# Two RWKV / mLSTM / sparse-attention layers on one core: waits of the feed-forward leads and of the RWKV projections rearranged

## What is computed

```python
for l in range(DEPTH):                                   # 2
    h = h + 0.5 * rms(swiglu(rms(h, g[0]), ffn_w_in[l, 0], ffn_w_out[l, 0]), g[1])
    u = rms(h, g[2])
    p_rw, p_ml, p_dsa, p_gate = split(u @ w_in[l])
    y_rw  = rwkv7_mixer(p_rw, ...)                        # lerp with the previous token, LoRAs, recurrence
    y_ml  = mlstm_mixer(p_ml, ...)
    y_dsa = dsa_mixer(p_dsa, ...)
    mixed = sum(sigmoid(p_gate) * (y @ w_branch[l])) @ w_out[l]
    h = h + rms(mixed, g[3])
    h = h + 0.5 * rms(swiglu(rms(h, g[4]), ffn_w_in[l, 1], ffn_w_out[l, 1]), g[5])
return h[:, 16:]
```

## Time and profile before

| | us |
|---|---|
| median of three timed runs | 3420.24 |
| lowest and highest | 3418.71, 3427.62 |
| profiled execution, its own time | 3413.78 |
| its span in the profile | 3412.1 |
| TensorE busy | 3272.8 |
| VectorE, ScalarE, GpSimd busy | 1475.8, 1178.8, 1193.5 |

### The profile page before, as it was taken

One profiled execution on the slowest core, in us unless ns is written; L12 is line 12 of the kernel. 1 busy time (PEld: TensorE's weight loads), 2 busy tenths in 40 slices (PEclk: granted clock), 3 DMA queues, 4 the chain that ended last, 5 costly groups with the idle time before them and its releaser, 6 DMA issues. The chain is left out here.

```text
span 3412.1 us, 72944 instructions
## 1 busy us (share of the span) xinstructions
PE 3272.8 (96%) x29406; PEld 3003.0 (88%) x29406; DVE 1475.8 (43%) x2548; ACT 1178.8 (35%) x2251; POOL 1193.5 (35%) x906
## 2 busy tenths in 40 slices
PE   8999999999899999999999999999898989999998
PEld 8999989987688999999999999999776868878886
DVE  6332155345767434332053311454467673353312
ACT  3222242224554334222232223513245543332222
POOL 4444345110002443444444443352000124534442
PEclk9999999998999999999999999999899999999999
DMA  3333222002111332333223332220021213323332
GB/s 101 89 92 89 79 69 69 5 9 56 42 51 39 85 93 70 90 92 88 80 84 89 92 90 85 63 62 4 18 54 39 59 29 98 87 81 94 93 94 70
DMA packets 464405, 236.48 MB, mean 69 GB/s; under 512 B 20862, under 2 KB 462476, under 8 KB 464156
## 3 DMA queue, kind: packets, MB, share of 16 engines
q1 hardware_dynamic: 464156, 232.92, 24.4%
HBM read 230.50 MB, written 2.10 MB: 68 GB/s over the span
## 5 line engine op out<-in xcount | busy, mean ns | idle before, releaser
L579 POOL TENSOR_TENSOR W_low<-W,W_high 128x512 fp32r<-128x512 f32 (+1 forms) x544 | 725.2, 1335 | 868.6 <-ACT W_high L659 867.8
L155 PE MATMUL PS<-u_high,W_high 128*128 128x264 f32 (+1 forms) x2832 | 864.1, 305 | 8.5 <-DVEq L458 3.4
L156 PE MATMUL PS<-u_low,W_high 128*128 128x264 f32 (+1 forms) x2832 | 857.9, 303 | 0.0
L157 PE MATMUL PS<-u_high,W_low 128*128 128x264 f32 (+1 forms) x2832 | 857.7, 303 | 0.0
L659 ACT ACTIVATE W_high<-W 128x512 fp32r<-128x512 f32 (+1 forms) x544 | 336.0, 619 | 997.0 <-PE PS L157 943.6
L155 PEld LDWEIGHTS PS<-u_high,W_high 128*128 128x128 f32 x2832 | 533.2, 188 | 37.1 <-issue 6.3
L156 PEld LDWEIGHTS PS<-u_low,W_high 128*128 128x128 f32 x2832 | 533.7, 188 | 21.5
L157 PEld LDWEIGHTS PS<-u_high,W_low 128*128 128x128 f32 x2832 | 531.7, 188 | 21.7
L155 PE MATMUL PS<-u_high,dW_high 128*128 128x264 f32 (+1 forms) x1344 | 408.3, 304 | 12.4 <-POOL dW_low L1745 5.0
L157 PE MATMUL PS<-u_high,dW_low 128*128 128x264 f32 (+1 forms) x1344 | 386.1, 287 | 0.0
L156 PE MATMUL PS<-u_low,dW_high 128*128 128x264 f32 (+1 forms) x1344 | 386.0, 287 | 0.0
(11 more groups left out here) (399 smaller groups left out, 5333.5 us busy)
## 6 DMA issues: line engine op xcount, KB each, us to landing
W<-in_ffn_w_in SPq DMA_DIRECT2D x352, 256.0 KB, 2.9
dW<-in_w_in SPq DMA_DIRECT2D x172, 256.0 KB, 2.9
W<-in_ffn_w_out SPq DMA_DIRECT2D x160, 256.0 KB, 2.8
W<-in_w_in SPq DMA_DIRECT2D x80, 256.0 KB, 3.0
W<-in_w_branch SPq DMA_DIRECT2D x48, 256.0 KB, 2.9
W<-in_w_out SPq DMA_DIRECT2D x32, 256.0 KB, 2.8
W<-in_ffn_w_out SPq DMA_DIRECT2D x32, 128.0 KB, 2.2
xt<-in_x SPq DMA_DIRECT2D x4, 512.0 KB, 4.7
```

The lines of the kernel that those rows point to most:

```text
L155: nc.tensor.matmul(dst, wh, xh, start=first, stop=False)
L156: nc.tensor.matmul(dst, wh, xl, start=False, stop=False)
L157: return nc.tensor.matmul(dst, wl, xh, start=False, stop=final)
L579: g.tensor_tensor(WL[:, r, 0:nk], W[:, r, 0:nk], WH[:, r, 0:nk].bitcast(F32), ALU.subtract).then_inc(S("split"), 1)
```

## The change

In the feed-forward lead the banks of the sums and of the spread factors change places, tile 2 is made before the wait for the sums, and the third and fourth high halves are made behind the first and second k in place of ahead of them. In the RWKV projections the last eight tiles use four pairs of banks, the memsets come before the first low half, the kappa sums come four blocks (one unit) later, and PE waits for the fourth kappa scaling ahead of tile 15's last unit and the rest. The turn of the small tile, its copies and its transfer move into the first chunk of the recurrence, with bank 4 in place of bank 0; the slice function is renamed `at`.

```diff
@@ phase_ffn
-                lead = Lead(st, [hid[:, 0], hid[:, 1]], pre, (4, 6, 0), True)
+                lead = Lead(st, [hid[:, 0], hid[:, 1]], pre, (6, 4, 0), True)
...
                         pe.sem_inc(dve_evac, 4)
+                        tile(0, 2)
                         pe.wait_ge(S("sums_read"), 1)
-                        tile(0, 2)
                         tile(0, 3)
...
                         def first_high(act, k):
-                            for n in {None: (0, 1, 2, 3), 5: (4,), 6: (5,), 7: (6,)}.get(k, ()):
+                            for n in {None: (0, 1), 0: (2,), 1: (3,), 5: (4,), 6: (5,), 7: (6,)}.get(k, ()):
                                 high(n, n // R, n % R, 4)
@@ phase_rwkv, projections
-            dense = Dense(early, ..., columns, None, (4, 6, 2, 0) + (4, 6) * 10,
+            dense = Dense(early, ..., columns, None, (4, 6, 2, 0) + (4, 6) * 6 + (2, 0, 4, 6) * 2,
                           True, size=4)
...
                 def _(g):
-                    for u in range(8):
-                        dense.low(g, u)
                     g.memset(s3[:], 1.0).then_inc(S("starts"), 1)
                     g.wait_ge(S("starts"), 1)
                     g.memset(full(s3)[:, :, :, 0:1], 0.0)
                     g.memset(s3[:, :, NFULL * CH:NFULL * CH + 1], 0.0).then_inc(S("starts"), 1)
-                    for u in range(8, dense.all_units):
+                    for u in range(dense.all_units):
                         dense.low(g, u)
...
                     dense.blocks(pe, 4)
                     dense.blocks(pe, 4)
+                    dense.blocks(pe, 4)
                     pe.wait_ge(S("kappa_squares"), 1)
                     pe.wait_ge(S("sigmoid"), 8)
                     token_sums(lambda m: s4[:, m], per_parity, 2).then_inc(S("kappa_sums"), 1)
-                    dense.blocks(pe, 24)
+                    dense.blocks(pe, 20)
                     for m in range(4):
                         spread_out(m)
                         dense.blocks(pe, 8)
+                    pe.wait_ge(S("kappa_scaled"), 4)
                     dense.blocks(pe, KD * dense.tiles - dense.given)
-
-                    pe.wait_ge(S("d_out"), dense.tiles)
-                    pe.wait_ge(S("kappa_scaled"), 4)
-                    for j, (t0, n) in enumerate(QT):
-                        last = nc.tensor.transpose(PS[0:n, 0, 16 * j:16 * j + 16], small[64:80, t0:t0 + n],
-                                                   ident[64:80, 64:80])
-                    last.then_inc(S("small_turned"), 1)
@@ phase_rwkv, recurrence (the transfer and the two copies leave the projections too)
+                @block.sync
+                def _(sp):
+                    sp.wait_ge(S("small_turned"), 1)
+                    sp.dma_start(small[64:P], small[0:64]).then_inc(loaded2, 16)
+                    sp.wait_ge(loaded2, 16)
...
                             tt(za[:], near[:, :, 0], eye2[:].unsqueeze(1).broadcast_to([P, 4, 64]), ALU.add).then_inc(S("first_factor"), 1)
+                            if g == 0:
+                                v.wait_ge(S("small_turned"), 1)
+                                nc.vector.tensor_copy(tok[0:N_META, 0], PS[0:N_META, 4, 0:16])
+                                nc.vector.tensor_copy(tok[:, 1:5], PS[:, 4, 16:80].rearrange("p (j c) -> p j c", c=16)
+                                                      ).then_inc(S("small_out"), 1)
                             v.wait_ge(S("reach_made"), g + 1)
...
                         if p:
                             pe.wait_ge(S("x2"), p)
+                        else:
+                            pe.wait_ge(S("small_out"), 1)
...
                         if makes:
                             near_grams(g)
+                        if g == 0:
+                            turn_small()
                         if steps:
                             read(p)
```

More of the change, by code:

```diff
@@ L969, in phase_rwkv @@
                 ((0, C_KIDX, 72), (72, C_IG, 8))]
-            dense = Dense(early, w_in[ds(l, 1)].rearrange("a (k p) n -> p (a k) n", p=P), columns, None, (4, 6, 2, 0) + (4, 6) * 10,
+            dense = Dense(early, w_in[ds(l, 1)].rearrange("a (k p) n -> p (a k) n", p=P), columns, None, (4, 6, 2, 0) + (4, 6) * 6 + (2, 0, 4, 6) * 2,
                           True, size=4)
@@ L983, in _ @@
                         dense.load(sp, u)
-                    sp.wait_ge(S("small_turned"), 1)
-                    sp.dma_start(small[64:P], small[0:64]).then_inc(loaded2, 16)
-                    sp.wait_ge(loaded2, 16)
                 @block.gpsimd
                 def _(g):
-                    for u in range(8):
-                        dense.low(g, u)
                     g.memset(s3[:], 1.0).then_inc(S("starts"), 1)
@@ L1084, in _ @@
                         scaled(i)
-                    v.wait_ge(S("small_turned"), 1)
-                    nc.vector.tensor_copy(tok[0:N_META, 0], PS[0:N_META, 0, 0:16])
-                    own(nc.vector.tensor_copy(tok[:, 1:5], PS[:, 0, 16:80].rearrange("p (j c) -> p j c", c=16)))
                 @block.scalar
@@ L1239, in phase_rwkv @@
             LEN = [min(CH, T - g * CH) for g in range(NG)]
-            tok = lambda g: slice(g * CH, g * CH + LEN[g])
+            at = lambda g: slice(g * CH, g * CH + LEN[g])
             rows = lambda q, n: slice(64 * q, 64 * q + n)
@@ L1368, in grams @@
                                 for q in range(2):
-                                    last = mm(dst(m, k)[rows(q, n), 0:n], lhs[rows(q, 64), m, tok(g)],
-                                              rhs[rows(q, 64), m, tok(g)])
+                                    last = mm(dst(m, k)[rows(q, n), 0:n], lhs[rows(q, 64), m, at(g)],
+                                              rhs[rows(q, 64), m, at(g)])
                         return last
@@ L1377, in product, with turn_small @@
                         return last
+                    def turn_small():
+                        for j, (t0, n) in enumerate(QT):
+                            last = nc.tensor.transpose(PS[0:n, 4, 16 * j:16 * j + 16], small[64:80, t0:t0 + n],
+                                                       ident[64:80, 64:80])
+                        last.then_inc(S("small_turned"), 1)
                     def near_grams(g):
@@ L1395, in read @@
                             for q in range(2):
-                                last = mm(rps[rows(q, n), m], p_[rows(q, 64), m, tok(p)], state[rows(q, 64), s, m],
+                                last = mm(rps[rows(q, n), m], p_[rows(q, 64), m, at(p)], state[rows(q, 64), s, m],
                                           start=False)
@@ L1456, in turns @@
                                 for q in range(2):
-                                    last = mm(dst[rows(q, n), m], src[rows(q, 64), m, tok(g)], eye2[rows(q, 64)])
+                                    last = mm(dst[rows(q, n), m], src[rows(q, 64), m, at(g)], eye2[rows(q, 64)])
                         last.then_inc(S("turned"), 1)
@@ L1501, in outputs @@
                             for q in range(2):
-                                last = mm(yps[rows(q, 64), m, 0:n], state[rows(q, 64), s, m], r_[rows(q, 64), m, tok(p)],
+                                last = mm(yps[rows(q, 64), m, 0:n], state[rows(q, 64), s, m], r_[rows(q, 64), m, at(p)],
                                           start=False)
```

## The result

| | before | changed |
|---|---|---|
| median, us | 3420.24 (3417.41 to 3427.74, five runs) | 3395.59 (3386.33 to 3401.44, five runs) |
| ratio to before, 95% | | 0.9915 (0.9899 to 0.9931), 29 us faster |
| profiled execution, its span | 3413.78, 3412.1 | 3399.08, 3397.4 |
| TensorE busy | 3272.8 us, 96% | 3278.0 us, 96% |

A forecast was written before the change was run, and what follows sets the result against it. TensorE (PE), busy 96% of the span, was taken as the bound, so only its waits and slow clock could be won. Terms 3.4 + 10.1 - 0.5 + 2.2 + 2.8 + 5.6 + 2.4 = 26.0 us off 3420.2 gave 3394, range 3386 to 3406.

The forecast's parts named there:

- rival 1: Whole kernel: the forecast itself holds, 3394 us with its own range of 3387 to 3400; chance 0.50.
- Sums' banks: Feed-forward lead: tile 2 no longer waits for VectorE to read the sums; 4 x 0.86 = 3.4 us won.
- the margin of 1.8 us: Feed-forward lead: weights for tile 3's second half are ready 1.8 us before PE asks, however early the lead ends.
- Order of first splits: Feed-forward lead: two splits before the first `u_high` instead of four; 3 x 2.25 + 3.4 = 10.1 us won.
- without the wait I expect it to stay up: Very first feed-forward lead: without the 1.8 us wait the clock holds, adding 1.7 us for 3.4 in all.
- its lower end: Very first feed-forward lead: only the earlier PE start counts, 1.7 us instead of 3.4, without the clock gain.
- Memsets: RWKV stage start: GpSimd's memsets hold VectorE up 0.65 us in layer 2, save 0.1 twice; -0.5 us net.
- Kappa sums: RWKV projections: one 2.9 us unit goes ahead and covers PE's 1.1 us wait for the squares, twice; 2.2 us won.
- Bank pairs: Late RWKV projections: four pairs remove tile 19's 1.4 us wait per layer, GpSimd's low halves just keeping ahead; 2.8 us won.
- Small turn: End of RWKV projections: PE restarts at the recurrence 2.8 us sooner in each of two layers; 5.6 us won.
- The clock term: Recurrence restart: clock holds after a 1.5 us idle stretch, 1.5 won less 0.3 for transposes; net 1.2 a layer, 2.4 us.
- a gain under 14 us would prove the sum wrong in more than a size: Whole kernel: the prediction's own failure test, set against its summed gain of 26.0 us.

The follow-up runs named there:

- the second comparison: The changed kernel itself, timed again beside its feed-forward and RWKV halves, against the kernel before on the same chip: median 3391.73 us, ratio 0.9906.
- the idle stretch put back: The changed kernel plus a 128 KB transfer reloading unread weights, with a wait, at the end of the RWKV projections: 3403.23 us, against 3421.09 for the kernel before.

## Why the prediction was right, point by point

The forecast case, rival 1 of the list, is what happened: 3394 forecast, 3395.59 measured. That the two lie within 1.6 us is partly luck. The gain is 26 in the forecast, 24.7 between these two medians, 29 by their ratio and 32 in the second comparison, so the sum was right in its size and some 3 to 6 us too low.

- **Sums' banks**, 0.86 a stage. Right in what went, a little low in size: 1.1 to 1.3 alone, and the margin of 1.8 us before the second half of tile 3 held.
- **Order of first splits**, 2.25. Right: 2.25 to 2.49 alone in three of four stages. The step "without the wait I expect it to stay up", for the clock in the first lead, failed. The first lead lost clock in six of the seven profiles that have this edit and in five of the seven that have not, so taking the wait away did not save the clock. It did move the loss: with the edit the fall begins at 15.0 to 16.1 us (0.80 from 14.3 to 23), without it at 23.6 to 24.1 in four of the five, just behind the wait, and at 14.8 in one. What causes the early fall is open. The order alone gave 2.37 in the first stage for a forecast of 3.4, and with the banks the stage gave 3.3 to 3.6 instead of 4.26; with the idle stretch put back the clock happened to hold, and it gave 4.63. The term belonged nearer to its lower end. That the feed-forward edits as a whole still gave the 13.5 of the forecast (13.8 by stage lengths) is luck: the clock fell short by some 0.7, and the other three stages gave 10.2 for 9.3.
- **Memsets**, -0.5 forecast, near it: 0.85 lost in layer 2, at best 0.3 won in layer 1, and split 8's 0.1 won twice.
- **Kappa sums**, 2.2 forecast, 2.6 at equal clock, and some 2.4 through the clock that the sum did not hold. With the pairs this is why the RWKV edits gave 17.8.
- **Bank pairs**, 2.8 forecast, 3.3 measured. GpSimd's low halves kept ahead as argued: PE is busy for the whole window.
- **Small turn**, 5.6 forecast, 5.8 measured. The clock term, 1.2 a layer, was 1.46 where the clock held and some 0.6 where it did not, about 1.0 in the mean of the restarts. The recurrence as a whole varies by more (128.6 to 133.6 us over all profiles), which is the +3.2 of layer 2.

The sum by measured parts is 13.7 + 2.6 + 3.3 + 5.8 - 0.5 + some 2 for the restarts = 27, and 29 with the clock behind the kappa sums, where the two ratios say 29 and 32. The single step that failed, the clock in the first lead, is small, and a gain through the clock behind the kappa sums, which the sum did not hold, outweighs it. What the prediction did not foresee is that the profiled execution would show half of the gain. Some 5 us went in the stages behind the recurrences, 3 in the recurrence of layer 2, and 3 in the first feed-forward of layer 2, where the head ran 6.8 us at half clock. Its own test, "a gain under 14 us would prove the sum wrong in more than a size", applied to that one execution would have come within 1 us of a false alarm (14.7).

## What to carry to other kernels

Where one engine is busy 96% of the time, take its waits one at a time and ask of each what comes next and by what margin; here every removed wait gave its own length or a little more, and each margin had been read first. Judge such parts by segment lengths at equal granted clock, over several executions, and the whole by timed medians: one pair of profiles was off by half. When a wait is gone, look at the order of the engine that feeds the next; the last 2.8 us a layer were one split queued behind two copies that waited for something else.

## What the hardware showed that was not expected

- A VectorE operation on 14 columns, 0.17 us alone, was held for 1.85 us by a GpSimd memset of 1.86 us.
- Forty matmuls of two columns behind a stretch at 2.4 GHz are followed by 3.4, 6.8 or 10.2 us at 1.2 GHz, differing from execution to execution, while PE shows no pause.
- A pause of 1.45 us at a stage boundary left the clock at 2.4 GHz for the small matmuls behind it in eight of twelve restarts, and one of 4.0 us brought it to 0.52 and 0.50 of full speed in the two layers.
- The stage behind the recurrence takes 270 to 272 or 273 to 275 us with the same instructions, with 33 to 36 or 40 to 43 us at half clock.
